# Two-layer decoder on one core: every slab of weights fetched by two transfers of 64 partitions instead of one of 128

## What is computed

```python
DEPTH, D_MODEL, SEQ = 2, 2048, 256
PEER_EXPERTS, PEER_HEADS, PEER_TOPK = 16384, 8, 16

for layer in range(DEPTH):
    if layer % 2 == 0:
        x = x + even_mixer(rmsnorm(x, e_norm), e_w_in, ..., e_w_out)
    else:
        x = x + odd_mixer(rmsnorm(x, o_norm), o_w_in, ..., o_w_out)
    x = x + peer_ffn(rmsnorm(x, f_norm[layer]), f_w_q[layer], f_sub_keys[layer], f_u[layer], f_v[layer])
return rmsnorm(x, final_norm)

def peer_ffn(h, w_q, keys, u_tab, v_tab):
    # scores of h @ w_q against the keys, top 16 of each head -> expert numbers eid, weights g
    a = einsum('td,thkd->thk', h, u_tab[eid])
    coef = g * gelu(a)
    return einsum('thk,thkd->td', coef, v_tab[eid])
```

## Time and profile before

| | |
|---|---|
| median of 3 runs | 3772.84 us (3771.99 to 4657.47) |
| the profiled execution | 3771.17 us, of which 3769.3 us are the span from the first to the last instruction |
| granted TensorE clock | 0.997 |
| busy: PE, PEld (weight loads), DVE, ACT, POOL | 99%, 84%, 62%, 46%, 39% |
| moved by DMA | 806.96 MB, mean 214 GB/s |

### The profile page before, as it was taken

The page is one execution under the profiler, slowest core; times in us unless marked ns, Lnnn a source line. Parts: engine busy times, 40 slices in busy tenths (PEclk is TensorE's granted clock), DMA queues, the critical chain, the costliest instruction groups (busy, mean ns, idle before and its releaser), DMA issues.

```text
span 3769.3 us, 55569 instructions
## 1 busy us (share of the span) xinstructions
PE 3741.5 (99%) x18832; PEld 3179.9 (84%) x18832; DVE 2328.7 (62%) x3255; ACT 1736.4 (46%) x2120; POOL 1457.9 (39%) x1175
## 2 busy tenths in 40 slices
PE   8999999999999999999999999999999999999999
PEld 7998988888888888888899889888888888888887
DVE  4565777776555555555564657677875555555555
ACT  4354444444444444444454544444444444444444
POOL 2020188888841222222121000688888502222220
PEclk9999999999999999999999999999999999999999
DMA  6566798999986666666575666799899876666665
GB/s 224 185 206 209 221 211 217 216 216 216 216 227 222 221 222 220 221 220 220 181 222 174 215 222 179 200 216 217 217 216 217 228 221 219 222 222 225 227 220 193
DMA packets 373583, 806.96 MB, mean 214 GB/s; under 512 B 121073, under 2 KB 184753, under 8 KB 373089
## 3 DMA queue, kind: packets, MB, share of 16 engines
q1 hardware_dynamic: 279376, 758.34, 65.8%
q0 software_dynamic: 94096, 47.26, 8.8%
HBM read 732.76 MB, written 40.11 MB: 205 GB/s over the span
## 4 chain that ended last, share of the span: by engine, by line
PE 97%; DMA 1%; ACT 1%; DVE 1%; POOL 0%; issue 0%; SPq 0%; DVEq 0%; ACTq 0%
PE ps L2188 37%; PE ps L2137 37%; PE ps L1811 4%; PE ps L1816 4%; PE ps L1820 4%; PE ps L1897 4%; PE ps L1832 2%; PE ps L1838 1%; DMA w_raw<-in_dense 1%; PE ps L1884 1%; PE ps L2040 0%; PE ps L2124 0%; POOL big L588 0%; DVE w_lo L1222 0%; ACT w_hi L745 0%; ACT act_hi_t L861 0%
## 5 line engine op out<-in xcount | busy, mean ns | idle before, releaser
L1222 DVE TENSOR_TENSOR w_lo<-w_raw,w_hi 128x1024 fp32r<-128x1024 f32 x1312 | 1634.8, 1248 | 1368.9 <-ACT w_hi L745 1354.0
L745 ACT ACTIVATE w_hi<-w_raw 128x1024 fp32r<-128x1024 f32 x1312 | 1389.6, 1061 | 1851.8 <-DMA w_raw<-in_v_tab 759.9
L681 POOL DMA_INDIRECT weight_grid<-cv,idx x512 | 1040.9, 2033 | 260.5 <-issue 161.4
L699 POOL DMA_DIRECT2D gb<-weight_grid x480 | 256.8, 535 | 1158.6 <-PE ps L2188 1025.2
L2137 PE MATMUL ps<-w_hi,act_hi_t 128*128 128x512 f32 x2048 | 571.2, 390 | 0.1
L2137 PE MATMUL ps<-w_hi,act_lo_t 128*128 128x512 f32 x2048 | 568.5, 389 | 0.0
L2137 PE MATMUL ps<-w_lo,act_hi_t 128*128 128x512 f32 x2048 | 568.4, 389 | 0.0
L2188 PE MATMUL ps<-w_hi,act_hi_t 128*128 128x512 f32 x2048 | 552.6, 389 | 0.0
L2188 PE MATMUL ps<-w_lo,act_hi_t 128*128 128x512 f32 x2048 | 552.3, 389 | 0.0
L2188 PE MATMUL ps<-w_hi,act_lo_t 128*128 128x512 f32 x2048 | 552.2, 389 | 0.0
L2137 PEld LDWEIGHTS ps<-w_hi,act_hi_t 128*128 128x128 f32 x2048 | 381.7, 188 | 85.9 <-issue 5.0
(11 more groups left out here) (235 smaller groups left out, 2236.2 us busy)
## 6 DMA issues: line engine op xcount, KB each, us to landing
w_raw<-in_u SPq DMA_DIRECT2D x512, 512.0 KB
w_raw<-in_v_tab SPq DMA_DIRECT2D x512, 512.0 KB
w_raw<-in_dense SPq DMA_DIRECT2D x288, 512.0 KB
weight_grid<-gb SPq DMA_DIRECT2D x64, 512.0 KB, 5.2
gb<-weight_grid POOLq DMA_DIRECT2D x512, 64.0 KB, 3.8
big<-big SPq DMA_DIRECT2D x960, 32.0 KB
weight_grid<-cv,idx POOLq DMA_INDIRECT x512
x_spill<-big POOLq DMA_DIRECT2D x16, 256.0 KB, 4.8
```

The costliest lines, as they stand in the source:

```text
L681: pool.indirect_dma_start(grid, bass.IndirectOffsetOnAxis(ap=idx[:, n, k:k + 1], axis=0), cv[:, n, k:k + 1], None, compute_op=ALU.add).the ...
L699: pool.dma_start(dst, src).then_inc(s_gb[c % 2], 16)
L745: act.activation(w_hi[:, slot, :], w_raw[:, slot, :], ACT.Copy).then_inc(s_hi, 1)
L1222: dve.tensor_tensor(w_lo[:, slot, :], w_raw[:, slot, :], w_hi[:, slot, :].bitcast(F32), ALU.subtract).then_inc(s_lo, 1)
```

## The change

`PARTS = 2` is new. A load is issued as two transfers, partitions 0 to 63 and partitions 64 to 127 of the slab, one behind the other on SP, with the same wait ahead of the first and none between them. Each adds 16 to the slot's semaphore, and ScalarE waits for 32 for each slab where it waited for 16. Nothing else is different.

```diff
+PARTS = 2
...
                 if wait:
                     sp.wait_ge(s_used, n - (RING - 1))
-                sp.dma_start(w_raw[:, slot, :], src).then_inc(s_landed[slot], 16)
+                for p0 in range(0, P, P // PARTS):
+                    sp.dma_start(w_raw[p0:p0 + P // PARTS, slot, :], src[p0:p0 + P // PARTS, :]).then_inc(s_landed[slot], 16)
...
             def hi(slot, n):
 
-                act.wait_ge(s_landed[slot], (n // RING + 1) * 16 if isinstance(n, int) else (n - slot) * 4 + 16)
+                act.wait_ge(s_landed[slot], (n // RING + 1) * (16 * PARTS) if isinstance(n, int)
+                            else (n - slot) * (4 * PARTS) + 16 * PARTS)
                 act.activation(w_hi[:, slot, :], w_raw[:, slot, :], ACT.Copy).then_inc(s_hi, 1)
```

## The result

Every slab in halves of 64 partitions took 4017.73 us (median of 4 runs, 4012.28 to 4022.15), against 3773.4 us before: ratio 1.0652, 95% interval 1.064 to 1.0665, 6.5% slower. The ratio and its interval leave out the one execution of the kernel before that took 4657.47 us. The forecast was 3776 us with a range to 4000, so the time lies outside, on the side of rivals B and C.

What follows compares the result with a forecast made beforehand. TensorE's matmuls were taken to bound the kernel. SP's added issue counted nothing and late landings 3.4 us: 3771.17 + 3.4 = 3774.6, and with the median 1.7 above the profiled execution 3776 us, range 3765 to 4000.

Steps and rivals of the forecast that it cites:

- Rival B: All stages, slower: a half moves at half the rate, crowding the DMA engines; middle 3976 us; chance 0.36.
- rival C: U stage, slower: each half costs SP a shuffle's issue, work 3.08 us over 2.72; 3944 us; chance 0.05.
- The bound, the chain and TensorE's idle time: Whole kernel: matmuls fill 3741.5 of 3769.3 us, chain 97% TensorE, idle 27.8 us; loads can gain at most 0.7%.
- I take the load's own 0.34, the row of the same shape, and with the address 0.49 us: SP's queue: the added issue of a half costs as much as a whole load's, 0.49 us with address work.
- Sum on SP: nothing: U stage: SP's work rises from 2.01 to 2.50 us of 2.72, swallowed by its 0.71 us wait; V has room.
- The upper end that I gave the issue: SP's queue: half a load may cost, at the other end, as much as a shuffle, 0.63 us.
- the prediction's signs: If Rival B holds: U share goes to 1 below 217 GB/s, V share near 1 or well over 0.68.
- its upper form: All stages: a slab's transfer doubles from 1.35 to 2.70 us; U needs 3.47 us, V 2.87; 4223 us.
- Its lower form: Half of the crowding: U needs 2.79 us a slab, + 35 us, V fits; 3806 us; chance 0.07.
- The landing: Each slab: the second half is issued 0.49 us later, costing 0 to 0.49 us, hidden by slack of 1.44 or more.
- the places where no slab is in hand: Seven places, mostly turns of the dense stages, where the chain goes through a load: 0 to 3.4 us, 3.4 taken.
- case A: Whole kernel: no measurable change, the issue hidden by SP's wait and the landing by slack; 3776 us; chance 0.55.

Runs made afterwards that it cites:

- the kernels with whole slabs and extras: The kernel before, slabs whole, with two or one extra small SP transfers behind each U slab: 4037.23 us (1.071) and 3806.75 us (1.0092).
- SP relieved: The changed kernel, halves in all stages, but in the U stages ScalarE issues the second half (the first four U slabs of a layer excepted): 3814.16 us (1.0113).
- dv_halves: The kernel before with halves of 64 partitions in the V and dense stages only, U slabs whole: 3796.57 us (1.0077).

## Why the prediction was wrong

*The bound, the chain and TensorE's idle time.* Right. Nothing could be gained, and all that happened was that slabs came late.

*The step that failed: "I take the load's own 0.34, the row of the same shape, and with the address 0.49 us"*, and with it "Sum on SP: nothing". A load of 64 partitions was not of the same shape as one of 128 to SP. The forecast had SP's work for a U slab at 2.50 us; it was 3.19. The 0.69 is made of terms that the timelines show: two issues at 0.54 in place of 0.34, 0.40; the shuffles at 1.53 for the pair in place of 1.41, 0.12; 0.26 in place of 0.11 from the last shuffle to the next load, 0.15; the address between the halves 0.18 in place of 0.15. The 0.54 itself is the 0.47 of 64 partitions and 0.07 more that only the U stage shows; what makes the 0.07 is open. The 0.11 was a second, smaller error of mine: I had taken SP's work as 2.72 less the 0.71 us that it waits. Where SP does not wait, the gap reads 0.26 to 0.28, in the kernels with whole slabs and extras too. So part of it had been hidden under the wait, and the room was smaller than the view of waits said. Work of 3.19 against 2.72 over some 490 slabs is 230 us; the two U stages lost 228.5.

*The bound that was right, and its chance that was not.* The upper end that I gave the issue, a shuffle's 0.63, contains the 0.54, and rival C built on it named 3944 us and the signs that came: hardly a wait, a share that does not rise, issues of about 0.6. I gave it 0.05, on the ground that a load has not a shuffle's dimensions. That ground was a guess about what an issue costs, while the kernel's own rows held two unequal prices, 0.33 and 0.63, and no rule for them. With a room of 0.71 us and a cost between 0.49 and 0.78 on top of a first issue whose price could rise as well, the case deserved far more.

*Rival B.* Its mechanism is true and did not make the loss of the U stages, save perhaps for a part of the 22 us that are left with SP relieved. The rate of halves is 230 GB/s alone, the share of V rose to 0.87 as the prediction's signs had it, and V had 2.72 us for it. What the rival had too dear is the U stage: in its upper form it gave a slab 3.47 us of the engines, and with SP relieved a slab took 712.8 / 256 = 2.78 us. Its lower form, half of the crowding, had 2.79 us and 3806, near the 3814.16 of that kernel. But it put all of that into the U stages, while 27 us of the loss lie in the others, so the nearness is in part luck. What the Trainium skill's page SBUF — State Buffer, section "Door 1: The DMA port swizzle", says was borne out by the trace: its 196 GB/s for partitions 0 to 63 answer to 210 here, and its port map fits the 347 for partitions 32 to 95. The Trainium skill's page DMA: Bandwidth & Descriptors, section "Rules for kernel authors", was right in its advice to use one transfer of 128 partitions; the reason that it gives is the engines, and what decided here was the issuing queue.

*The landing, and the places where no slab is in hand.* The sum had 3.4 us; all but the U stages lost 27 us alone (dv_halves), and the chain of that kernel has 3% of loads where it had 1%. The term is right in kind and too small by far. The count of places was wrong: it was seven, and the chain of dv_halves goes through 19 loads, eight of them in the V stages, where the kernel before had none. The delay of a place was probably too small too: the engines take 2.28 us for a slab in halves and not 1.26, which I had left out of case A. No run parts the two.

*The range* ended at 4000, 18 us short. I had set its end by cutting off the top of B; C, at 3944 by my price, played no part in it. With C's price as measured (3.19 us a slab, 230 us) and the 27 us of the other stages the sum is 3771.17 + 230 + 27 = 4028, and the range would have had to reach there.

## What to carry to other kernels

Count the issuing queue as an engine: add up for one turn of the loop what each transfer costs it, in its own shape, with the gaps as they are when it never waits, and compare that with the turn of the engine that bounds. The waits of this queue overstated its room (0.71 us, of which some 0.15 was work once it did not wait). Below the turn an extra issue is nearly free (0.4% for two full-width transfers), above it the excess is paid in every turn; a split that keeps all 128 partitions, or issuing from another engine, moves the kernel back under it.

## What the runs showed of the hardware

An issue on SP costs by shape in no simple order: 0.328 us for 128 partitions, 0.465 for 64, 0.31 for 96, 32 and 16, and 0.51 for partitions 32 to 95 (0.53 in the V stage). The bytes don't matter: with 128 partitions 64 columns cost as 1024. In bursts of eight an issue costs 0.10 to 0.13 us more, and a half in the U stage 0.54. A burst to partitions 0 to 63 moved 210 GB/s, one to 32 to 95 347, one to all 128 415, and one to all 128 in halves of columns 346.
